# ScalarE's counters opened first, and the C factors of all blocks formed at once, in the front of a two-block sequence kernel

## The chip, the cores and the metric

One core of a Trainium2 chip (trn2) runs the whole kernel. The time is the device time of one execution in microseconds; the number compared is the median over runs. The engines are named PE (TensorE), DVE (VectorE), ACT (ScalarE), POOL (GpSimd) and SP (SyncE, which only issues DMAs here); "PEld" is PE's loading of weights.

## What is computed

A sequence of 512 tokens of width 1024 passes through two stacks of two layers. The change touches the start of the first layer, a state-space mixer, whose core is

```python
hn = rmsnorm(h, norm_mix[0])
dt = exp(log_dt)[:, None]; mag = exp(lam_re * dt)
a_r = mag * cos(lam_im * dt); a_i = mag * sin(lam_im * dt)
coef = ((a_r - 1) + 1j * a_i) / (lam_re + 1j * lam_im)   # coef_r, coef_i
bb = coef * (b_re + 1j * b_im)                            # 64 groups x 64 states x 16
# per group: s[t] = a * s[t-1] + bb @ hn[t];  y[t] = Re(c @ s[t])
y = gelu(y + d * hn); a, b = split(y @ w_glu); mix = a * sigmoid(b)
```

What follows (the gated feed-forward layers, windowed attention, a second stack with a second state-space layer and differential attention) isn't touched; it is 289 weight units of 128 x 1024 that stream from HBM while PE multiplies.

## The kernel before

Everything is written in one program, with one instruction stream for each engine and semaphores between them. There is no planner: each engine executes its list in the order of the code, and a wait stops all that stands behind it on that engine. `Steps` is a counter: a semaphore with a list of names, each of which is one increment a turn. So that the waits for a turn before the first are met, every counter has to be opened: `open(e)` adds 4 turns in advance. The engine that makes a counter's steps opens it.

The front works on 64 groups in 8 blocks (NBLK) of 8 groups (GB). The recurrence over 512 tokens is cut into 64 pieces (NSTEP) of 8 steps (STEP): tables with the powers 0 to 8 of each group's factor carry eight steps at once, and a scan over the 64 pieces does the rest.

- **Powers.** `s5_vector` (DVE) forms dt, the turns, and PB, the powers 0 to 8 of all groups (L578 to L604); ACT does the exponentials and sines in between (`s5_scalar`, L482 to L488). psi (L604) releases `psi_ready`, for which POOL waits.
- **B side.** DVE multiplies the first block's B by the norm's gain (L651); POOL does so for the other seven blocks, 896 elements twice (L453). `tables(q)` in `s5_vector` forms TB of block q (L614, L622, L623, L622, L623), and waits for `s5_k` "K2" of block q-1: TB is a single buffer, and PE's `direct(q-1)` reads it.
- **C side.** `c_powers(lo, hi)` (L635 to L647) forms TA, the factors of C, for a range of groups, in six instructions: L641, L642 and L644 and L645 read two operands in SBUF; L643 and L646 have one in PSUM. Before the change it is called for the first block (72 elements an instruction) and, behind U, for the other seven (504 elements). Each call ends with an increment of `tables_ready`. POOL's `tables(q)` (L427, L428, L429; 1152 elements each) forms TC of block q; the first waits for `tables_ready` 1, all others for 2.
- **The picked norm.** ACT squares h (L493), PE sums over the partitions (L739), ACT takes the root sd (L244). DVE picks from sd what each of the eight steps needs (L671, L673, L674) as ru, and U = Ur * ru of block 0 (L678). For blocks 1 to 7 POOL forms U (`inputs`, L434), and SP reloads Ur (L409) once U of the block before is done.
- **Angles.** POOL's `angles(q)` (L438) forms psi x piece number; DVE takes the fraction (`fractions`, L632, L633), ACT the sines and cosines (L500 to L504). `angles(0)` waits for psi, for the constants, and for the counter `s5_angles`, which ACT opens.
- **Blocks.** On DVE a block is L700, L702, L703, the scan L707, L709, `direct` (L689), L714, L716, then `tables` and `fractions` of the next one. On PE: `transposed` (L749), `step_sums` (L768: U through the turned tables), `rotated` (L774, needs ACT's copy L521 of the sums), `direct` (L759, needs TC), then outputs (L812, L813) and the turn of the scan's result (L795).

POOL's list at the start is: wait for psi; `angles(0)`; gain B; wait for C; `tables(0)`; then for T from 0: `tables(T + 1)`, `inputs`, `angles(T + 1)`.

Of the kernel before, what the change touches and what calls it, by code (L numbers as in the profile page):

```python
# [14 lines left out]
SG, SH, SN = 64, 16, 64  # L15
STEP = 8
NSTEP = TOK // STEP
GB = LANES // SH
# [74 lines left out]
def program(nc, a):  # L93
    ctx = ExitStack()
    with ctx:
# [10 lines left out]
        def sem(name):  # L106
            return ctx.enter_context(nc.semaphore(name))
# [30 lines left out]
        def V(name, lo=0, hi=None, rows=LANES):  # L138
            a0, a1 = PC[name]
            return par[0:rows, a0 + lo:(a1 if hi is None else a0 + hi)]  # L140
# [48 lines left out]
        def act_split(e, v0, n4):  # L189

            if isinstance(n4, int) and v0 + 4 * n4 >= UNITS:
                return
            z = v0 % RING
            e.wait_ge(raw_loaded[z], n4 * 16 + (v0 // RING + 1) * 16)
            e.activation(w_hi[:, z], raw[:, z], ACT.Copy).then_inc(hi_split, 1)  # L195
# [44 lines left out]
        def act_norm(e, n, eps):  # L240
            e.wait_ge(norm_mm, n + 1)
            if n:
                e.wait_ge(r_ready, n)
            e.activation(sd[:, :], bk[4], ACT.Sqrt, bias=eps[:, :], scale=1.0 / DM).then_inc(sd_ready, 1)  # L244
# [101 lines left out]
        s5_kept = Steps(sem("s5_kept"), "Sx", ahead=4)  # L346
        s5_st_kept = Steps(sem("s5_turned_kept"), "ST1 ST2", ahead=4)
        s5_k_kept = Steps(sem("s5_direct_kept"), "K1 K2", ahead=4)
        s5_angles = Steps(sem("s5_angles"), "absf sin cos", ahead=4)
        s5_y_kept = Steps(sem("s5_y_kept"), "Y1 Y2", ahead=4)  # L350
        s5_gelu = Steps(sem("s5_gelu"), "hi g", ahead=4)
# [10 lines left out]
        def link(e, ins):  # L362

            chain[0] += 1
            ins.then_inc(vec_chain, 1)
            e.wait_ge(vec_chain, chain[0])
# [16 lines left out]
        def cut(t, q, width=GB):  # L383

            return t[:, q * width:(q + 1) * width]
# [91 lines left out]

        def s5_scalar(e):
            s = small
            flat = lambda t: t[:, :, :].rearrange("p g s -> p (g s)")  # L480
            e.wait_ge(par_loaded, 16)
            e.activation(s["dt"][:, :], V("log_dt"), ACT.Exp).then_inc(dt_ready, 1)  # L482
            e.wait_ge(magnitudes, 1)
            e.activation(flat(power["mag"]), flat(power["mag"]), ACT.Exp).then_inc(magnitudes, 1)
            e.wait_ge(power_steps, 1)
            e.activation(flat(power["sin"]), flat(power["turns"]), ACT.Sin, scale=SIN_SCALE).then_inc(trig_ready, 1)
            e.wait_ge(power_steps, 2)
            e.activation(flat(power["cos"]), flat(power["whole"]), ACT.Sin, bias=half_pi[:, :], scale=-SIN_SCALE).then_inc(trig_ready, 1)  # L488
            e.wait_ge(h_loaded, 16)
            for m in range(KT):  # L490
                if m >= 4:
                    e.wait_ge(acc_ready, m - 3)
                e.activation(squares[m % 4], h[:, m], ACT.Square).then_inc(squared, 1)  # L493
            act_norm(e, 0, eps6)

            def turned(t):
                z = t % 2
                e.wait_ge(s5_phases.sem, s5_phases.at("f", t))
                e.wait_ge(s5_angles.sem, s5_angles.at("cos", t - 1))
                s5_angles.took("absf", e.activation(absf, ff, ACT.Abs))  # L500
                e.wait_ge(s5_states.sem, s5_states.at("po2", t - 2))
                s5_angles.took("sin", e.activation(sinb[:, z], ff, ACT.Sin, scale=SIN_SCALE))
                e.wait_ge(s5_angles.sem, s5_angles.at("absf", t))
                s5_angles.took("cos", e.activation(cosb[:, z], absf, ACT.Sin, bias=half_pi[:, :], scale=-SIN_SCALE))  # L504

            def st_kept(t):
                e.wait_ge(s5_sums.sem, s5_sums.at("S", t - 1))
                for k in (1, 2):
                    e.wait_ge(s5_tt.sem, s5_tt.at(f"ST{k}", t))
                    s5_st_kept.took(f"ST{k}", e.activation(ST[:, 4 * k - 4:4 * k, :], bk[k - 1].rearrange("p (g n) -> p g n", g=4), ACT.Copy))  # L510

            def k_kept(t):
                e.wait_ge(t_loaded[t % 2], 16 * STEP * (t // 2 + 1))
                for k in (1, 2):
                    e.wait_ge(s5_k.sem, s5_k.at(f"K{k}", t))
                    s5_k_kept.took(f"K{k}", e.activation(Ksb[:, t % 2, 4 * k - 4:4 * k, 1:, :], kbank(k)[:, :, 1:, :], ACT.Copy))

            def s_kept(t):
                e.wait_ge(s5_sums.sem, s5_sums.at("S", t))
                e.wait_ge(s5_js.sem, s5_js.at("JS", t - 2))  # L520
                s5_kept.took("Sx", e.activation(Sx[:, t % 2], grid(bank[2]), ACT.Copy))  # L521

            def step(T):
                if 0 <= T < NBLK:
                    st_kept(T)
                    if T == 0:
                        turned(T)
                        s_kept(T)
                    k_kept(T)
                q = T - 2  # L530
                if 0 <= q < NBLK:
                    e.wait_ge(s5_turned.sem, s5_turned.at("YT", q))
                    tok = bk[7].rearrange("p (s c) -> p s c", s=STEP)
                    s5_gelu.took("hi", e.activation(cut(x1h, q, 1).rearrange("p o (c s) -> p (o s) c", s=STEP), tok, ACT.Gelu_apprx_tanh))
                    e.wait_ge(s5_low.sem, s5_low.at("lo", q - 1))
                    s5_gelu.took("g", e.activation(a32[:, :], bk[7], ACT.Gelu_apprx_tanh))
                if 0 < T < NBLK:
                    s_kept(T)
                    turned(T)
                q = T - 1  # L540
                if 0 <= q < NBLK:
                    e.wait_ge(s5_turned.sem, s5_turned.at("YT", q - 1))
                    for k in (1, 2):
                        e.wait_ge(s5_out.sem, s5_out.at(f"Y{k}", q))
                        s5_y_kept.took(f"Y{k}", e.activation(Ysb[:, :, 4 * k - 4:4 * k, :].rearrange("p s g h -> p g s h"), ybank(k).rearrange("p (g s h) -> p g s h", g=4, s=STEP), ACT.Copy))
                if 3 <= T < 6:
                    act_split(e, T - 3, 0)
            for counters in (s5_kept, s5_st_kept, s5_k_kept, s5_angles, s5_y_kept, s5_gelu):
                counters.open(e)
            for T in range(NBLK + 2):  # L550
                step(T)
            e.wait_ge(par_rest, 16)
            e.wait_ge(const_rest, 16)
            e.sem_inc(x_hi, 8)

        def kbank(k):
            return bank[5][64 * (k - 1):64 * (k - 1) + SH, :].rearrange("p (g s h) -> p g s h", g=4, s=STEP)

        def ybank(k):
            return bank[4][64 * (k - 1):64 * k, :]  # L560

        def s5_vector(e):
# [72 lines left out]
            def c_powers(lo, hi):  # L635

                p0, p1 = PB[:, 0, lo:hi], PB[:, 1, lo:hi]
                wr, ci = over(v("w")[:, lo:hi]), over(v("ci")[:, lo:hi])
                m0, m1 = (b[:, 0:(hi - lo) * (STEP + 1)].rearrange("p (g s) -> p g s", s=STEP + 1) for b in (bank[6], bank[7]))
                t0, t1 = TA[:, 0, lo:hi], TA[:, 1, lo:hi]  # L640
                link(e, tt(m0, p0, wr, ALU.mult))  # L641
                link(e, tt(t0, p1, ci, ALU.mult))  # L642
                link(e, tt(t0, m0, t0, ALU.add))  # L643
                link(e, tt(m1, p0, ci, ALU.mult))  # L644
                link(e, tt(t1, p1, wr, ALU.mult))  # L645
                link(e, tt(t1, t1, m1, ALU.subtract))  # L646
                e.sem_inc(tables_ready, 1)  # L647
# [14 lines left out]
            link(e, tt(v("c2"), v("nr"), v("g2"), ALU.mult))  # L662
            link(e, tt(v("ci"), v("c3"), v("c2"), ALU.subtract))
            c_powers(0, GB)
            link(e, ts(mag8[:, :], mag[:, :, STEP], 1.0, None, ALU.mult))
            e.wait_ge(const_loaded, 16)
            fractions(0)
# [8 lines left out]
            e.sem_inc(ru_ready, 1)  # L676
            e.wait_ge(u_loaded, 16)
            s5_inputs.took("U", tt(Ub[:, 0], Ur[:, :, :], ru[:, :].unsqueeze(1).to_broadcast(full), ALU.mult))  # L678
            c_powers(GB, SG)
            dg = bank[7][0:SH, 0:SG]  # L680
            link(e, tt(dg, V("d_h", rows=SH), V("gain_u", rows=SH), ALU.mult))
            dfull = [SH, SG, SH]
# [1907 lines left out]
```

## Time and profile before

| | |
|---|---|
| Median of 3 runs | 2085.6 us (2083.46 to 2087.68) |
| Profiled execution | 2085.45 us, span 2083.7 us |
| PE busy | 1944.7 us (93%) |
| DVE busy | 1279.2 us (61%) |
| ACT busy | 898.9 us (43%) |
| POOL busy | 433.5 us (21%) |
| Mean granted clock of PE | 0.973 |
| PE busy in each of the first four slices of 52 us, in tenths | 3, 8, 7, 9 |
| PE's granted clock in these slices, in tenths | 7, 8, 9, 9 |

The profile is of one execution. A row of the time order gives the start, the length, engine and line, what is written and read with shapes, and in brackets how long the engine had been idle before it and what released it. A length includes time in which the instruction had begun and was held up. Where a row says "x8", it is eight instructions in a row. PE is busy nearly everywhere but in the first 160 us, the front, where the work is handed from engine to engine.

### The profile page before, as it was taken

To read this page: it belongs to the slowest core of one execution; us is meant where nothing else is said; L and a number is where in the kernel's file an instruction comes from. 1 tells how busy PE (TensorE), PEld (TensorE's weight loads), DVE (VectorE), ACT (ScalarE), POOL (GpSimd) and SP (SyncE) were. 2 spreads that over 40 slices of the span, in tenths; PEclk is the share of its full clock that TensorE was granted. 3 is DMA by queue.
4 is the path that set the end of the run, shared out by engine and by line. 5 is a ranking of instruction groups with operands and counts; after the bars stand their busy time and mean duration, and the time that the engine had idled before them with its cause. 6 is when DMAs were issued, how large, how long until landed. Compare 5 with 4: busy or idle time off the path is not lost.

```text
span 2083.7 us, 27291 instructions
## 1 busy us (share of the span) xinstructions
PE 1944.7 (93%) x9494; PEld 1564.5 (75%) x9494; DVE 1279.2 (61%) x1783; ACT 898.9 (43%) x1503; POOL 433.5 (21%) x295
## 2 busy tenths in 40 slices
PE   3879999999999967999999999999999998999996
PEld 2668788888887745788888887878878886777774
DVE  7984443433469587543343468987667765777764
ACT  3674432332335255432232333445445552466661
POOL 4772200000044010300000044352212224100003
PEclk7899999999999979999999999999999999999998
DMA  4213333333332200332333332222222222222221
GB/s 178 45 33 108 94 91 101 93 98 99 93 99 84 84 6 11 91 100 91 101 93 99 96 96 81 81 61 63 70 79 64 71 71 62 91 62 62 70 71 61
DMA packets 54522, 166.98 MB, mean 80 GB/s; under 512 B 13216, under 2 KB 13344, under 8 KB 53920
## 3 DMA queue, kind: packets, MB, share of 16 engines
q1 hardware_dynamic: 54432, 165.78, 26.6%
q8 instruction: 56, 0.92, 0.2%
q14 instruction: 34, 0.28, 0.0%
HBM read 161.30 MB, written 2.10 MB: 78 GB/s over the span
## 4 chain that ended last, share of the span: by engine, by line
PE 74%; DVE 12%; ACT 5%; POOL 3%; issue 3%; DMA 2%; DVEq 0%; POOLq 0%; SPq 0%; PEldq 0%
PE bank L183 15%; PE bank L184 15%; PE bank L185 15%; PE bank L1478 3%; PE bank L1479 3%; PE bank L1480 3%; DMA raw<-in_w_dram 2%; PE bank L2084 2%; PE bank L2086 2%; PE bank L2085 2%; PE bank L1493 1%; POOL acc L234 1%; PE bank L1494 1%; PE bank L1495 1%; ACT w_hi L195 1%
## 5 line engine op out<-in xcount | busy, mean ns | idle before, releaser
L203 DVE TENSOR_TENSOR w_lo<-raw,w_hi 128x1024 fp32r<-128x1024 f32 x286 | 367.2, 1284 | 460.8 <-ACT w_hi L195 459.4
L195 ACT ACTIVATE w_hi<-raw 128x1024 fp32r<-128x1024 f32 x289 | 305.8, 1058 | 627.2 <-DMA raw<-in_w_dram 627.2
L183 PE MATMUL bank<-x1h,w_hi 128*128 128x512 f32 x744 | 291.6, 392 | 6.6 <-DVE x1l L218 6.6
L185 PE MATMUL bank<-x1h,w_lo 128*128 128x512 f32 x744 | 289.7, 389 | 0.0
L184 PE MATMUL bank<-x1l,w_hi 128*128 128x512 f32 x744 | 289.7, 389 | 0.0
L183 PE MATMUL bank<-x0h,w_hi 128*128 128x512 f32 x704 | 277.9, 395 | 0.0
L185 PE MATMUL bank<-x0h,w_lo 128*128 128x512 f32 x704 | 274.1, 389 | 0.0
L184 PE MATMUL bank<-x0l,w_hi 128*128 128x512 f32 x704 | 274.0, 389 | 0.0
L232 POOL TENSOR_TENSOR sq<-h 128x512 f32 (+1 forms) x64 | 79.0, 1234 | 784.0 <-DVEq L917 660.4
L183 PEld LDWEIGHTS bank<-x1h,w_hi 128*128 128x128 f32 x744 | 139.7, 188 | 38.1 <-DVE x1l L218 7.9
L184 PEld LDWEIGHTS bank<-x1l,w_hi 128*128 128x128 f32 x744 | 139.8, 188 | 29.3 <-issue 0.7
L185 PEld LDWEIGHTS bank<-x1h,w_lo 128*128 128x128 f32 x744 | 139.8, 188 | 29.1
L1478 PE MATMUL bank<-x1h,w_hi 128*128 128x512 f32 x384 | 155.9, 406 | 0.0
L183 PEld LDWEIGHTS bank<-x0h,w_hi 128*128 128x128 f32 x704 | 132.2, 188 | 29.8 <-issue 2.5
L184 PEld LDWEIGHTS bank<-x0l,w_hi 128*128 128x128 f32 x704 | 132.2, 188 | 29.3 <-issue 2.3
L185 PEld LDWEIGHTS bank<-x0h,w_lo 128*128 128x128 f32 x704 | 132.1, 188 | 27.5
L1479 PE MATMUL bank<-x1l,w_hi 128*128 128x512 f32 x384 | 151.1, 393 | 0.0
L1480 PE MATMUL bank<-x1h,w_lo 128*128 128x512 f32 x384 | 150.9, 393 | 0.0
L234 POOL TENSOR_TENSOR acc<-acc,sq 128x512 f32<-128x512 f32 x64 | 102.5, 1602 | 5.0
L896 DVE TENSOR_TENSOR x1l<-a,x1h 128x512 f32 x64 | 44.3, 693 | 92.7 <-ACT a L886 92.7
L884 ACT ACTIVATE x1h<-t 128x512 f32 x64 | 40.5, 632 | 130.7 <-DVE t L894 130.7
L1478 PEld LDWEIGHTS bank<-x1h,w_hi 128*128 128x128 f32 x384 | 73.1, 190 | 18.1 <-issue 1.9
(379 smaller groups left out, 3464.7 us busy)
## 6 DMA issues: line engine op xcount, KB each, us to landing
raw<-in_w_dram SPq DMA_DIRECT2D x289, 512.0 KB, 3.5
h<-in_xT_dram SPq DMA_DIRECT2D x1, 2048.0 KB, 12.6
Ur<-in_xu_dram SPq DMA_DIRECT2D x8, 256.0 KB, 2.7
out_dram<-h SPq DMA_DIRECT2D x8, 256.0 KB, 2.2
const<-in_const_dram SPq DMA_DIRECT2D x1, 1028.0 KB, 14.6
B_st<-in_B_dram SPq DMA_DIRECT2D x1, 1024.0 KB, 6.8
C_st<-in_C_dram SPq DMA_DIRECT2D x1, 1024.0 KB, 14.6
p_in<-in_pT_dram SPq DMA_DIRECT2D x1, 1024.0 KB, 5.1
```

The lines of the kernel that those rows point to most:

```text
L183: e.matmul(b, w_hi[:, w, k], xh[:, k], start=(k == 0), stop=False)
L184: e.matmul(b, w_hi[:, w, k], xl[:, k], start=False, stop=False)
L185: last = e.matmul(b, w_lo[:, w, k], xh[:, k], start=False, stop=(k == KT - 1))
L195: e.activation(w_hi[:, z], raw[:, z], ACT.Copy).then_inc(hi_split, 1)
L203: e.tensor_tensor(w_lo[:, z], raw[:, z], w_hi[:, z].bitcast(F32), ALU.subtract).then_inc(w_split, 1)
L232: e.tensor_tensor(one(sq[:, :]), tile(h, m), tile(h, m), ALU.mult).then_inc(squared, 1)
L234: e.tensor_tensor(acc[:, :], acc[:, :], sq[:, :], ALU.add).then_inc(acc_ready, 1)
L896: e.tensor_tensor(tile(x1l, m), one(a32[:, :]), tile(x1h, m).bitcast(F32), ALU.subtract).then_inc(a_ready, 1)
L1478: e.matmul(b, w_hi[:, w, k], x1h[:, k], start=(k == 0), stop=False)
L1479: e.matmul(b, w_hi[:, w, k], x1l[:, k], start=False, stop=False)
L1480: last = e.matmul(b, w_lo[:, w, k], x1h[:, k], start=False, stop=(k == KT - 1))
L2084: e.matmul(b, w_hi[:, w, k], xh[:, k], start=(k == 0), stop=False)
```

## The change

ScalarE opens its six counters as the first thing it does, instead of after the norm's root. And DVE forms the C factors of blocks 1 to 7 (`c_powers(GB, SG)`) right after those of block 0, instead of behind U of block 0: ahead of the copy mag8 (L665), the fractions of block 0 and the picked norm.

```diff
@@ s5_scalar(e):
             s = small
+            for counters in (s5_kept, s5_st_kept, s5_k_kept, s5_angles, s5_y_kept, s5_gelu):
+                counters.open(e)
             flat = lambda t: t[:, :, :].rearrange("p g s -> p (g s)")
             e.wait_ge(par_loaded, 16)
...
                 if 3 <= T < 6:
                     act_split(e, T - 3, 0)
-            for counters in (s5_kept, s5_st_kept, s5_k_kept, s5_angles, s5_y_kept, s5_gelu):
-                counters.open(e)
             for T in range(NBLK + 2):
                 step(T)
@@ s5_vector(e):
             c_powers(0, GB)
+            c_powers(GB, SG)
             link(e, ts(mag8[:, :], mag[:, :, STEP], 1.0, None, ALU.mult))
             e.wait_ge(const_loaded, 16)
             fractions(0)
...
             s5_inputs.took("U", tt(Ub[:, 0], Ur[:, :, :], ru[:, :].unsqueeze(1).to_broadcast(full), ALU.mult))
-            c_powers(GB, SG)
             dg = bank[7][0:SH, 0:SG]
```

No instruction is added or removed.

## Rows read from the trace of the kernel before

**Rows 1.** The page: the span of the profiled execution.

```profile
span 2083.7 us, 27291 instructions
```

**Rows 2.** The chain of work that ended last: start us, length us, engine, output, line.

```profile
30.97 0.89 DVE Ub L678
...
56.06 1.54 DVE Zb L707 x8
```

**Rows 3.** POOL in order of time, 0 to 75 us: start, length, instruction, idle before.

```profile
25.75 1.04 POOL L438 TENSOR_TENSOR R<-psi,const 128x512 f32<-128x512 f32 x1 [23.20 <-ACTq L64]
26.75 4.56 POOL L453 TENSOR_TENSOR B_st<-B_st,gain_row 128x896 f32<-128x896 f32 x2
31.27 2.59 POOL L427 TENSOR_TENSOR TC<-C_st,TA 128x1152 f32<-128x1152 f32 x1
...
36.47 2.94 POOL L429 TENSOR_TENSOR TC<-TC,TCt 128x1152 f32<-128x1152 f32 x1
41.53 2.14 POOL L427 TENSOR_TENSOR TC<-C_st,TA 128x1152 f32<-128x1152 f32 x1 [2.12 <-DVEq L647]
```

**Rows 4.** DVE in order of time, 0 to 75 us.

```profile
12.75 0.43 DVE L651 TENSOR_TENSOR B_st<-B_st,gain_row 128x256 f32<-128x256 f32 x1 [0.23 <-DVE psi L604]
13.21 1.23 DVE L614 TENSOR_TENSOR TB<-B_st,PB 128x1024 f32<-128x1024 f32 x1
14.35 0.69 DVE L622 TENSOR_TENSOR bank<-B_st,PB 128x512 f32<-128x512 f32 x1
...
21.18 0.22 DVE L665 TENSOR_SCALAR mag<-s_mag 128x64 f32<-128x64 f32 x1 [0.16 <-DVE TA L646]
...
28.26 1.13 DVE L671 TENSOR_TENSOR bank<-sd,const 128x512 f32<-128x512 f32 x1
...
30.27 0.55 DVE L674 RECIPROCAL ru<-ru 128x64 f32<-128x64 f32 x1
...
31.78 2.62 DVE L641 TENSOR_TENSOR bank<-PB,s_w 128x504 f32<-128x504 f32 x1
...
40.71 0.68 DVE L646 TENSOR_TENSOR TA<-TA,bank 128x504 f32<-128x504 f32 x1
41.55 2.21 DVE L681 TENSOR_TENSOR bank<-par 16x64 f32<-16x64 f32 x1 [0.15 <-DVE TA L646]
...
45.03 1.94 DVE L614 TENSOR_TENSOR TB<-B_st,PB 128x1024 f32<-128x1024 f32 x1
46.89 3.10 DVE L622 TENSOR_TENSOR bank<-B_st,PB 128x512 f32<-128x512 f32 x1
...
69.80 0.70 DVE L702 TENSOR_TENSOR bank<-bank,sinb 128x512 f32<-128x512 f32 x1 [1.38 <-PE bank L774]
```

**Rows 5.** ACT in order of time, 25 to 26.5 us.

```profile
25.33 0.69 ACT L244 ACTIVATE sd<-bank,eps 128x512 f32<-128x512 f32 x1 [1.59 <-PEq L741]
```

**Rows 6.** DMA: C on the page, then Ur's tile, 0 to 60 us.

```profile
C_st<-in_C_dram SPq DMA_DIRECT2D x1, 1024.0 KB, 14.6
...
DMA to landing us min/median/max: 2.6/3.5/13.0
```

**Rows 7.** DVE in order of time: two one-source instructions, early and late.

```profile
4.92 0.20 DVE L583 TENSOR_SCALAR s_k<-s_k 128x64 f32<-128x64 f32 x1
...
1854.83 1.07 DVE L2237 TENSOR_SCALAR s2t_nm<-s2t_mx 128x2 f32<-128x2 f32 x1
```

**Rows 8.** POOL in order of time, 1805 to 2012 us.

```profile
1854.57 1.31 POOL L2332 TENSOR_TENSOR ol<-OT,oh 128x512 fp32r<-128x512 f32 x1 [77.65 <-ACT oh L2284]
```

**Rows 9.** PE in order of time, 0 to 75 us.

```profile
31.91 3.67 PE L768 MATMUL bank<-Ub,ST 128*128 128x64 f32 x16 [5.28 <-DVE Ub L678]
36.28 2.07 PE L774 MATMUL bank<-Sx,const 128*128 128x512 f32 x2 [0.69 <-ACT Sx L521]
39.46 2.72 PE L759 MATMUL bank<-TC,TB 128*16 128x128 f32 x16 [1.11 <-POOL TC L429]
```

**Rows 10.** PE in stretches of 0.2 us: us, busy (x), clock, DMA share, GB/s.

```profile
67.80:68.00 0.20, 0.20 (x3) 0.51 0.00 0
```

## The prediction

> **What bounds the kernel now.** The program spans 2083.7 us [rows 1]; all that the change touches happens in its first 60. I read the chain of work first: it says which part of the front can give or cost time. From 30.97 us, where VectorE scales the first block's input (U, L678), to the scan of block 0 that ends at 57.60 us, nearly every piece is VectorE's [rows 2]; the scan L707 is in the chain again in each later block. So a delay of the scan of block 0 is a delay of the end: weight loads, splits and the PE-bound remainder all follow in relative order.
>
> Second, POOL's row of time. It sat idle 23.20 us until ScalarE's queue (L64, the counters' increment) let it start L438 at 25.75, then gained B for 4.56 us, then formed the first block's C tables (L427 to L429) from 31.27 and the second's from 41.53 [rows 3]. The reader is to see that all this work is dammed up behind one increment.
>
> Third, VectorE's row beside it [rows 4]. L641 takes 2.62 us, L622 3.10 us, and L681, of 16x64 elements, 2.21 us; L622 alone at 14.35 took 0.69. The long ones read both sources from SBUF while POOL is at work, and end just after POOL's instruction ends: L427 ends at 31.27 + 2.59 = 33.86, L641 at 34.40; L453 ends at 31.31, U at 31.86 [rows 2 to 4]. So one of the two engines waits out the other's whole instruction, and VectorE then needs another 0.54 us for 512 elements (0.08 for the 64 of L681, some 1.08 for the 1024 of L614: 1.23 - 0.69 + 0.54). It is mutual: the second L453 ends 31.31 - 29.39 = 1.92 us after L671 let it go, and L427 33.86 - 31.86 = 2.00 us after U; free, it takes 2.14 [rows 3, 4]. For L429, 2.94 less some 0.45 of waiting is 2.5. The two alternate. L646, with a source in PSUM, takes 0.68 beside POOL [rows 4].
>
> The Trainium skill (SBUF — State Buffer, section "Who interferes with whom") says the same: a VectorE instruction with two SBUF inputs and a GpSimd instruction that reads SBUF block each other wholly, in order of issue. It speaks against this change, which starts POOL sooner.
>
> **The counters opened first.** The six increments move ahead of ScalarE's wait for the parameters and cost nothing on the path. The transposes no longer wait for them behind sd (25.33 + 0.69 = 26.02 [rows 5]), worth nothing, as U comes later. POOL is now released when psi is ready, at 12.75 - 0.23 = 12.52 us [rows 4]: it starts L438 at 12.67 (it woke 0.14 us after L646's end at 41.39 [rows 3, 4]), ending 13.71, against VectorE's gain L651, ready at 12.75. L651 ends 13.98; POOL's first L453 15.90; L614 16.98; the second L453 18.90; the first L622 19.44, where it ended at 15.04 before. From there POOL waits for the C powers and VectorE runs free. Cost: **+4.4 us** up to this point. Before, it was hidden: VectorE idled for the angles until 26.9 anyhow. C lands 14.6 us after its issue [rows 6], which is among the first on SP's queue: in time.
>
> **The C powers ahead.** The small powers ended at 21.18 - 0.16 = 21.02, now 25.42. This starts POOL's tables(0) at 25.56 (5.7 us earlier), and the large powers at 25.58. They took 31.78 to 41.39 = 9.6 us, six instructions worth some 4.3 free, the rest waiting for exactly these POOL instructions [rows 3, 4]. The same company is there now: L427 25.56 to 27.70, L641 to 28.24; from L641's end to L646's took 41.39 - 34.40 = 6.99, so L646 ends at 35.23. Moving them removes no contention.
>
> **What now stands before U.** The increment after L646 wakes POOL for tables(1) at 35.37; the copy L665 (mag8) starts at 35.38. L665 reads one source, SBUF to SBUF. No such copy stands beside POOL in the front, so I bound it: 0 more if it does not wait (the reciprocal L674, also of one source, ran its 0.55 us within L453 [rows 3, 4]), 2.1 if it waits out L427. The nearest row is of its own operation: L2237, of 2 elements, began at 1854.83 within POOL's L2332 (from 1854.57, 1.31 long) and took 1.07, ending 0.02 after it [rows 7, 8]. I take the wait. What speaks against it is that L665's source is strided: its 0.22 us [rows 4] is more than L583's 0.20 for as many contiguous elements [rows 7], so it could run in another form.
>
> The Trainium skill (VectorE: DVE Perf Modes, section "Mode 2×_2P — use both read ports for one tensor") wants for the two-port mode only SBUF on both sides and an even outermost dimension, 64 here, and no unit stride. By that L665 waits: 2092.3 below; by a strided form that does not wait, 2089.6.
>
> L665 ends at 37.6; the two fractions instructions (1.4) at 39.0; L671 waits for L428 (37.6 + 2.14 = 39.73) and ends at 40.3; from L671's end to U's start took 30.97 - 29.39 = 1.58 [rows 2, 4], so U stands ready at 41.87, waits for L429 (40.3 + 2.5) and ends at **43.3**, against 31.86: **+11.4**. ScalarE's angles of block 0, behind the fractions, are done by then and have room.
>
> **From U to tables(1).** TB is a single buffer: tables(1) on VectorE waits until PE's direct(0) has read TB. PE's chain from U: 31.91 step sums, 36.28 turn (after ScalarE's copy), 39.46 direct(0), done at 42.18, of which 1.1 was a wait for POOL's TC [rows 9], gone now. So 31.86 to 42.18 less 1.15 is 9.2: direct(0) is done at 43.3 + 9.2 = **52.5**. Before, L614 started at 45.03, led by VectorE itself with 2.9 us to spare; now PE leads it. This is the wait that takes the place of the powers: VectorE has nothing left but L681 and L683 (to 44.7) and then idles.
>
> POOL: tables(1) ends at 42.8; inputs(1) needs the reload of Ur, which SP issues behind U (landing 2.6 at the least [rows 6]): 46.0 to 47.3 (L438, of equal size, takes 1.04 free; the L434 in this place 1.3); angles(1) to 48.35; then tables(2), three instructions from 48.35: L427 to 50.5, L428 to 52.7. L614 arrives at 52.5 and ends 52.7 + 1.08 = 53.8; L429 takes it to 56.3; the first L622 ends at **56.8**. Before it ended at 46.89 + 3.10 = 49.99 [rows 4]: tables(1) met POOL both times. Difference **+6.8 us**. The rest up to the scan of block 0 had no waits for POOL before and has none after. POOL has done tables(2) earlier, so that L709 is shorter by up to 1.8, but PE, from this scan on, sets the next step: L702 waited 1.38 us for PE's turn [rows 4], and does so again.
>
> **The sum.** The profiled execution took 2085.45 us (span 2083.7 and 1.75 around it); the median of the three runs is 2085.6. 2085.45 + 6.8 = **2092.2**, 0.32% over the median.
>
> **The rivals.** (1) *The wait of L665 does not happen.* U ends at 40.6, direct(0) at 49.8, tables(2) on POOL starts at 45.6, and the first L622 ends at 54.05: +4.1, 2089.6. For it: the strided source. Chance 0.12, half of it above 0.2%.
>
> (2) *PE's clock.* The granted clock is at its lower level, 0.5 (1.2 GHz), in the whole stretch from 31 to some 68 us [rows 10], and L768's 16 matmuls take 3.67 us [rows 9]. After the change PE's first burst is without the 1.1 us hole. Should it rise in it and stay, PE's step after the scan shortens and VectorE can gain the 1.38 and the shorter L709: some 2.8, so +4.0, 2089.5. It speaks against it that VectorE's idle time leaves PE idle for some 5 us after direct(0). Chance 0.13, half below 0.2%.
>
> (3) *The change does what it seems to be after:* VectorE and POOL overlap freely where they were not seen together, in the gaining of B and the early tables(0). The powers take 4.3 us from 21.2 and end near 25.5, before sd (26.02 [rows 5]); fractions, L671 to L674 and U end near 30.3; direct(0) is done at 39.5; tables(1) takes 3.5 us free and ends at 43.1, where it ended near 52.4: -9.3, 2076. It decides if L614 at 14.0 does not wait for L453. Everything in [rows 3, 4] speaks against. With partial forms of it (-4 and more) chance 0.12.
>
> (4) *Partly absorbed*, 0 to +4: POOL in another rhythm, for instance free when L622 comes (it then ends at 54.4 or sooner). Chance 0.10.
>
> (5) *More than forecast:* Ur lands 3.5 us after its issue [rows 6], POOL's L428 ends at 53.5, and the first L622 at 57.6: +7.6, and with one POOL instruction more in VectorE's way up to +9.5, 2095. Chance of over +8: 0.08.
>
> **How the numbers follow.** Forecast (+6.3 to +8) 0.45, rivals 0.12, 0.13, 0.12, 0.10, 0.08. The range 2086.8 to 2095.0 holds the forecast, rivals 1 and 2, half of 4 and most of 5: about 0.8. About 0.2% is what a measurement of this kernel can tell from no change, here 4.2 us. Slower: 0.45 + 0.06 + 0.06 + 0.08 = 0.65; faster 0.12; within 0.2%: 0.23.
>
> **What the profile after would show.** POOL's L438 at 12.7 instead of 25.75; L614 of 3.0 and L622 of 2.4 us near 14 to 19.5; POOL's first L427 near 25.6; L665 of 2.2 us; U near 43; L614 of tables(1) near 52.5 with an idle time ended by PE's L759; the first block's scan near 64. L665 of 0.2 us would be rival 1; L614 of 1.2 us at 14 rival 3; a granted clock of 1.0 before 60 us rival 2. The prediction is wrong if tables(1) starts before 45 us, or if the shift at the first scan isn't found at the end.

## The result, and the profile after

The changed kernel took 2093.66 us, median of 7 runs (2089.85 to 2095.42), against 2086.56 for the kernel before (7 runs): a ratio of 1.0028, 95% interval 1.0015 to 1.0041. It is slower, as forecast, and inside the range; the forecast was 2092.2. The profiled execution spans 2091.9 us, 8.2 more than [rows 1].

The page of the changed kernel, its first lines:

```profile
span 2091.9 us, 27291 instructions
...
PE 1948.7 (93%) x9494; PEld 1570.5 (75%) x9494; DVE 1284.5 (61%) x1783; ACT 898.9 (43%) x1503; POOL 434.5 (21%) x295
```

Some lines of code have moved by one or two: L665 is now L666, L671 is L672, L678 is L679, L504 is L506. POOL in order of time, the counterpart of [rows 3] (start, length, instruction, idle before and its releaser):

```profile
12.64 1.04 POOL L438 TENSOR_TENSOR R<-psi,const 128x512 f32<-128x512 f32 x1 [10.09 <-DVEq L605]
13.64 5.27 POOL L453 TENSOR_TENSOR B_st<-B_st,gain_row 128x896 f32<-128x896 f32 x2
25.63 2.65 POOL L427 TENSOR_TENSOR TC<-C_st,TA 128x1152 f32<-128x1152 f32 x1 [6.72 <-issue]
...
35.22 2.14 POOL L427 TENSOR_TENSOR TC<-C_st,TA 128x1152 f32<-128x1152 f32 x1 [1.39 <-DVEq L647]
```

POOL starts 13.1 us sooner. DVE in order of time, the counterpart of [rows 4]:

```profile
12.72 1.23 DVE L651 TENSOR_TENSOR B_st<-B_st,gain_row 128x256 f32<-128x256 f32 x1 [0.23 <-DVE psi L604]
13.99 2.98 DVE L614 TENSOR_TENSOR TB<-B_st,PB 128x1024 f32<-128x1024 f32 x1
16.89 2.58 DVE L622 TENSOR_TENSOR bank<-B_st,PB 128x512 f32<-128x512 f32 x1
...
25.59 0.69 DVE L641 TENSOR_TENSOR bank<-PB,s_w 128x504 f32<-128x504 f32 x1 [0.16 <-DVE TA L646]
26.32 2.50 DVE L642 TENSOR_TENSOR TA<-PB,s_ci 128x504 f32<-128x504 f32 x1
...
35.24 2.19 DVE L666 TENSOR_SCALAR mag<-s_mag 128x64 f32<-128x64 f32 x1 [0.16 <-DVE TA L646]
...
41.72 1.43 DVE L679 TENSOR_TENSOR Ub<-Ur,ru 128x512 f32<-128x512 f32 x1 [0.15 <-DVEq L677]
...
52.44 1.23 DVE L614 TENSOR_TENSOR TB<-B_st,PB 128x1024 f32<-128x1024 f32 x1 [7.91 <-PE bank L759]
53.58 3.11 DVE L622 TENSOR_TENSOR bank<-B_st,PB 128x512 f32<-128x512 f32 x1
...
62.53 1.53 DVE L707 TENSOR_TENSOR_SCAN Zb<-mag,bank 128x64 f32<-128x64 f32 x8
...
74.56 0.70 DVE L702 TENSOR_TENSOR bank<-bank,sinb 128x512 f32<-128x512 f32 x1 [1.39 <-PE bank L774]
```

The reader is to see three things. POOL's L438 (12.64 to 13.68 us) stretches L651 by 0.80 us, and its two instructions that gain B stretch L614 and L622 by 1.75 and 1.89, 4.4 together. The copy mag8 takes 2.19 us where it took 0.22. And DVE idles for 7.91 us before tables(1), released by PE's L759: the wait that took the place of the powers. The scan of block 0 starts at 62.53, 6.5 us later than in [rows 2].

The chain of work that ended last (start, length, what) shows the same hand-over to PE between U and tables(1):

```profile
41.72 1.44 DVE Ub L679
...
43.20 3.69 PE bank L768 x16
...
46.92 0.60 ACT Sx L523
...
47.57 2.07 PE bank L774 x2
49.64 2.60 PE bank L759 x15
```

**Where the 8.2 us of the profile are.** I followed three marks through both traces: the start of the scan of block 0, the start of block 1's scan, and POOL's memset L226 that starts the norm in the GLU. They stand at 56.06, 71.26 and 163.01 us before and at 62.53, 76.03 and 172.80 after: later by 6.5, 4.8 and 9.8 us. At the last norm the shift is 8.2. So the front up to the scan explains 6.5; PE's step behind it gave back 1.7; the stretch from block 1's scan to the GLU took 5.0 more; and some 1.6 came back after it. The stretch from 60 to 170 us, PE alone, of before and then of after (us, busy (x), granted clock, DMA share, GB/s):

```profile
60.00:170.00 110.00, 91.57 (x670) 0.96 0.17 38
```

```profile
60.00:170.00 110.00, 96.05 (x647) 0.85 0.17 37
```

The mean granted clock there is 0.85 instead of 0.96; it drops to 0.5 (1.2 GHz) for part of several blocks. From scan to scan the kernel before has a clock of 1.00 everywhere behind its second scan. The changed kernel has 0.76 from the third scan to the fourth (14.2 us instead of 13.4), 0.75 from the fifth to the sixth (13.7 instead of 13.5) and 0.60 from the seventh to the eighth (12.2 instead of 10.4). The two stretches that follow the last two of these are at 1.00 and 0.99 and still take 0.6 and 1.7 us more, so over 2 of the 5.0 us fall behind a low stretch and not in it. At the last block, where DVE waits for PE's sums and ACT's angles, the row of L700 shows it: it had waited 4.15 us before and 5.73 after, and PE's step sums had taken 3.52 us at the lower level where they take 1.9 at the upper.

```profile
155.32 0.69 DVE L700 TENSOR_TENSOR tA<-bank,cosb 128x512 f32<-128x512 f32 x1 [5.73 <-ACT cosb L506]
```

### The profile page after: what moved, and what is told of

Same layout as the page of the kernel before. It is cut to its first block, busy times and chain, and to the rows that moved or that the text cites. A ratio compares the mean times of both kernels' runs of the same rounds, so it can differ in the third digit from the quotient of the medians.

```text
span 2091.9 us, 27291 instructions
## 1 busy us (share of the span) xinstructions
PE 1948.7 (93%) x9494; PEld 1570.5 (75%) x9494; DVE 1284.5 (61%) x1783; ACT 898.9 (43%) x1503; POOL 434.5 (21%) x295
## 4 chain that ended last, share of the span: by engine, by line
PE 74%; DVE 11%; ACT 5%; issue 3%; POOL 3%; DMA 2%; DVEq 0%; POOLq 0%; SPq 0%; PEldq 0%
PE bank L183 15%; PE bank L185 15%; PE bank L184 15%; PE bank L1478 3%; PE bank L1480 3%; PE bank L1479 3%; DMA raw<-in_w_dram 2%; PE bank L2084 2%; PE bank L2086 2%; PE bank L2085 2%; POOL acc L234 1%; PE bank L1493 1%; PE bank L1494 1%; PE bank L1495 1%; ACT w_hi L195 1%
## 6 DMA issues: line engine op xcount, KB each, us to landing
const<-in_const_dram SPq DMA_DIRECT2D x1, 1028.0 KB, 14.2
```

## The experiments

All columns but the last are read from one profile of each kernel; "scan" is the start of block 0's scan, "GLU mark" the start of L226. The last column compares the medians with the kernel before on the same chip, over 7 to 12 runs of the kernel and 7 to 31 of the kernel before.

| Kernel | U ends | Scan of block 0 | GLU mark | Scan to mark | Clock, 60 to 170 us | Ratio to before (95%) |
|---|---|---|---|---|---|---|
| before | 31.86 | 56.06 | 163.01 | 106.95 | 0.96 | 1 |
| changed | 43.15 | 62.53 | 172.80 | 110.27 | 0.85 | 1.0028 (1.0015 to 1.0041) |
| changed, again | 43.17 | 62.56 | 170.44 | 107.88 | 0.88 | 1.0031 (1.0016 to 1.0046) |
| counters only | 30.89 | 52.18 | 159.14 | 106.96 | 0.98 | 0.9978 (0.9962 to 0.9994) |
| powers only | 31.48 | 52.89 | 165.33 | 112.44 | 0.89 | 0.9990 (0.9974 to 1.0007) |
| copy mag8 ahead | 40.78 | 60.23 | 165.51 | 105.28 | 0.97 | 1.0009 (0.9989 to 1.0029) |
| release after both | 35.27 | 53.35 | 159.48 | 106.13 | 0.95 | 0.9971 (0.9954 to 0.9989) |
| B gained later | 37.85 | 58.10 | 168.15 | 110.05 | 0.88 | 1.0002 (0.9987 to 1.0016) |
| all three | 31.86 | 52.90 | 165.30 | 112.40 | 0.87 | 0.9969 (0.9952 to 0.9986) |
| split gain | 32.07 | 50.16 | 158.18 | 108.02 | 0.94 | 0.9985 (0.9969 to 1.0002) |
| before, delayed | 32.32 | 64.41 | 176.14 | 111.73 | 0.82 | 1.0050 (1.0032 to 1.0067) |
| changed, filler | 43.17 | 62.62 | 166.86 | 104.24 | 0.96 | 1.0017 (1.0000 to 1.0035) |
| before, filler | 31.66 | 55.86 | 162.93 | 107.07 | 1.00 | 0.9991 (0.9972 to 1.0010) |

### Each part alone

Counters only (the second part undone):

```diff
             s = small
+            for counters in (s5_kept, s5_st_kept, s5_k_kept, s5_angles, s5_y_kept, s5_gelu):
+                counters.open(e)
```

> The kernel before with only the counters opened first; the large C powers stay behind U. Theory (VectorE and POOL wait out each other's whole instructions): the gaining of B still meets tables(0) and costs 4.4 us, but then U of block 0 ends near 33.4 us (31.9 before, 43.2 in the changed kernel), the powers behind it run free in 4.3 us instead of 9.6, and the scan of block 0 ends near 55 us, some 2.4 earlier than before (57.6; changed kernel 64.1). Rival (early POOL work is what costs, whatever the place of the powers): the scan ends 4 to 6 us later than before, at 62 or later. Whole time by the theory -2 us against before, give or take what PE's granted clock does later; by the rival +4 or more.

Measured: the scan starts at 52.18, 3.9 us earlier than before, and the whole is faster by 0.22% (2083.46 against 2087.85 us). The rival falls: early POOL work alone does not cost. DVE in order of time:

```profile
16.85 2.58 DVE L622 TENSOR_TENSOR bank<-B_st,PB 128x512 f32<-128x512 f32 x1
...
25.56 0.22 DVE L665 TENSOR_SCALAR mag<-s_mag 128x64 f32<-128x64 f32 x1 [0.16 <-DVE TA L646]
...
29.94 0.95 DVE L678 TENSOR_TENSOR Ub<-Ur,ru 128x512 f32<-128x512 f32 x1 [0.15 <-DVEq L676]
30.81 3.11 DVE L641 TENSOR_TENSOR bank<-PB,s_w 128x504 f32<-128x504 f32 x1
33.95 0.68 DVE L642 TENSOR_TENSOR TA<-PB,s_ci 128x504 f32<-128x504 f32 x1
```

The 4.4 us at B are paid here too, but in time that was idle. I had U end at 33.4 and it ended at 30.9: the copy mag8 began at 25.56, 0.03 before POOL's L427 (25.59), and so escaped. Behind U the powers ran nearly free: one wait of 2.4 us instead of 5.3 in all.

Powers only (the first part undone):

```diff
             c_powers(0, GB)
+            c_powers(GB, SG)
...
-            c_powers(GB, SG)
             dg = bank[7][0:SH, 0:SG]
```

> The kernel before with only the large C powers moved ahead; the counters are opened late, so that POOL stands still until 25.75 us. Theory: tables(0) on VectorE ends at 17.2 as before, the powers run free from 21.2 to 25.5 us (no instruction over 0.8 us), fractions and U stay where they were (U ends near 31.9), direct(0) is done near 41.1, and the scan of block 0 ends near 55 us, 2.5 earlier than before. Rival (the powers ahead of the norm delay U and with it everything): U ends near 36 and the scan near 62. Whole time by the theory -2.5 us against before, by the rival +4.

Measured: the powers ran free from 21.19 to 25.48, U ended at 31.48, and the scan started at 52.89, 3.2 us earlier than before. The copy mag8 was caught by L438, which ran from 25.38 to 26.42:

```profile
25.63 0.87 DVE L666 TENSOR_SCALAR mag<-s_mag 128x64 f32<-128x64 f32 x1 [0.16 <-DVE TA L646]
```

The whole is not to be told from before (0.9990): in its profile the stretch from scan to GLU took 112.4 us at a clock of 0.89, which ate the 3.2. That is one execution, 2.1 us above the median of its ten.

So each part alone brings the scan 3 to 4 us forward, and both together put it 6.5 us back. Together they start POOL's tables(0) at the very moment of the large powers, with U behind them. And both spend the same idle time of DVE, which before stood ahead of the fractions of block 0:

```profile
26.92 0.69 DVE L632 TENSOR_SCALAR bank<-R 128x512 f32<-128x512 f32 x1 [5.52 <-POOL R L438]
```

The 4.4 us at B fit into these 5.5 alone, and so do 4.3 us of powers without waits; together they don't.

### Which meeting costs what

The copy ahead of the powers, in the changed kernel:

```diff
+            link(e, ts(mag8[:, :], mag[:, :, STEP], 1.0, None, ALU.mult))
             c_powers(0, GB)
             c_powers(GB, SG)
-            link(e, ts(mag8[:, :], mag[:, :, STEP], 1.0, None, ALU.mult))
```

> The changed kernel with the copy mag8 moved ahead of both calls of the C powers, so that it no longer stands beside POOL's tables(1). Theory (the strided one-source copy waits out L427, 2.19 us in the changed kernel's profile, and U behind it then misses one more POOL instruction): U ends near 40.7 instead of 43.2, the scan of block 0 starts near 59.9 instead of 62.5. Rival (the 2.2 us would have been waited anyway at the next two-source instruction): the scan starts at 62 to 62.5.

Measured: U at 40.78 and the scan at 60.23, 2.3 us earlier than in the changed kernel (2.6 expected). A copy of 64 elements costs 2.3 us of the front by its place; the rival falls.

POOL released after both calls:

```diff
                 link(e, tt(t1, t1, m1, ALU.subtract))
-                e.sem_inc(tables_ready, 1)
...
             c_powers(GB, SG)
+            e.sem_inc(tables_ready, 2)
```

> The changed kernel with POOL's tables(0) released only after both calls of the C powers. Theory: the large powers run free (4.3 us instead of 9.6, from 25.6 to 29.9), POOL's tables(0) starts near 30 instead of 25.6, U ends near 37.9, and the scan of block 0 starts near 58.1 (62.5 in the changed kernel). Rival (the later tables(0) on POOL holds back PE's direct(0) by as much as the powers gain): the scan starts at 62 or later.

Measured: the powers ran free from 25.51 to 29.79, and the scan started at 53.35, 9.2 us earlier than in the changed kernel (4.4 expected). The mechanism held, its size was twice mine: the copy mag8 began at 29.95, 0.03 before POOL's L427 (29.98), and escaped as well, so that U ended 7.9 us earlier (5.3 expected), and DVE's tables(1) met POOL in a better rhythm (L622 1.75 us instead of 3.11). The whole is 0.29% faster than before, though the 4.4 us at B are still in it.

B gained on POOL after its tables(0):

```diff
             angles(0)
-            e.wait_ge(g_loaded, 16)
...
             tables(0)
+            e.wait_ge(g_loaded, 16)
+            e.wait_ge(b_loaded, 16)
+            for part in range(2):
+                tt(B_st[:, part, GB:], B_st[:, part, GB:], gain_row[:, GB:], ALU.mult).then_inc(b_gained, 1)
```

> The changed kernel with POOL's gaining of B for blocks 1 to 7 moved behind its tables(0). Theory: VectorE's tables(0) meets only L438 and ends near 18.1 instead of 21.65, but L453 then stands beside the end of the large powers and the copy mag8; U ends near 38, the scan of block 0 starts near 59.1, 3.4 earlier than in the changed kernel. Rival (the waiting only moves to where L453 went): the scan starts at 62 or later.

Measured: L614 took 1.22 us at 14.04 again, U ended at 37.85 and the scan started at 58.10, 4.4 us earlier (3.4 expected). U gained 5.3 us: 3.6 at L614 and L622, 1.0 at the copy mag8, which now stood beside L453 and took 1.14 instead of 2.19, and the rest at L672 and U itself. POOL's gaining of B, now from 30.20 to 34.75 us, makes DVE wait some 0.9 us at the copy and 0.5 at L672.

All three together, the three diffs above in one kernel:

> The changed kernel with all three: the copy mag8 ahead, POOL's tables(0) released after both calls, B gained on POOL after tables(0). Theory: the large powers run free and end near 26.5, U ends near 32, the scan of block 0 starts near 53.4, 9 us before the changed kernel and 2.6 before the kernel before; the whole time lies some 3 us under the kernel before, give or take PE's granted clock. Rival (the early release of POOL isn't worth anything once it has been spread out; counters alone are as good): the scan starts no earlier than in the kernel with the counters alone, 52.2. Both can hold; a scan later than 56 would speak against the theory of the waits.

Measured: U at 31.86, the scan at 52.90 (53.4 expected), 9.6 us before the changed kernel, the whole 0.31% faster than before (2083.36 against 2090.07 us). It isn't earlier at the scan than the counters alone (52.18), so this part of the rival holds too: once U stands at 31 to 32, the next thing late is tables(1) against POOL's tables(1), where L614 took 2.58 and L622 3.10 us.

This kernel and the late release split the 11.3 us by which U is late in the changed kernel. The late release takes away 7.9, most of what the meetings with tables(0) and tables(1) cost. The other 3.4 go when the waits at B go as well: 4.4 at B and 4.3 of powers are 3.2 more than the idle 5.5 us.

### The carry to the end

The kernel before with a pure delay:

```diff
+            for again in range(6):
-            link(e, tt(DI[:, :, :], ...
+                link(e, tt(DI[:, :, :], ...
```

> The kernel before with VectorE's product DI (L683) written six times instead of once, with the same values, just ahead of tables(1): a pure delay of some 6.2 us on VectorE in the place where the changed kernel is late, with POOL and the C powers as they were. Theory (a shift of the scan of block 0 is carried to the end): the scan starts near 62.5 us as in the changed kernel, and the median lies 5 to 7 us over the kernel before, like that of the changed kernel. Rival (the changed kernel's excess comes from something else of it, and the front has slack of its own): the scan is late but the median lies within 2 us of the kernel before.

Measured: the scan at 64.41, 8.4 us late where some 6.4 were expected (the six writes took 7.44, and tables(1) then met POOL three times), and the median 9.2 us over the kernel before (2097.18 against 2088.03), a ratio of 1.0050. A delay of the first scan without any of the change is carried to the end. The rival falls.

The changed kernel, unaltered:

> The changed kernel, unaltered, beside the others on one chip. Theory: the first scan starts at 62.5 us again, since nothing up to there depends on chance; from the scan to the GLU it takes between 104 and 112 us, the more the longer the granted clock is low in between, so that the median comes out 4 to 8 us over the kernel before. Rival (the low stretches of its first profile belong to the change): from scan to GLU it takes 110 us again.

Measured: U at 43.17 and the scan at 62.56, within 0.03 us of the first profile; the GLU mark at 170.44, 2.4 us earlier than there; the median 5.4 us over before. Up to the scan the two profiles agree. From scan to mark it took 107.9 us this time and 110.3 the first, so at least this difference isn't the change's own.

That a shift is carried to the end doesn't say that all of it arrives. With the copy ahead the scan is 4.2 us late and the median 0.45 under the kernel before, at a ratio of 1.0009 with an interval from 0.9989 to 1.0029; with all three the scan is 3.2 early and the median 6.7 under.

### The clock

The filler, one product that nothing reads, in the changed kernel and in the kernel before:

```diff
                 if 0 <= q < NBLK:
+                    e.matmul(bank[5][32:48, :], C("ident", hi=16), h[:, 0], start=True, stop=True)
                     e.wait_ge(s5_states.sem, s5_states.at("Z", q))
```

> The changed kernel with one more 128x16 by 512 product on PE in each block of the front, into a part of a PSUM bank that nothing reads, just before PE's wait for the scan (an idle stretch). Theory of the clock (of the 8.2 us between the two profiles only 4.8 stand at the second block, the rest comes from stretches at the lower granted clock in blocks 3 to 8): with the filler the granted clock stays at 1.0 from the third block to the GLU, and the GLU's start (POOL's memset L226) is near 168 us instead of 172.8 (163.0 before). Rival (the later 5 us have another cause, a queue or a weight load): the clock may rise, the GLU still starts near 172 or later.

> The kernel before with the same filler. It was at clock 1.0 from 68 us on in its profile, so by the theory of the clock its front changes by under 1 us there, GLU's start near 163, and its runs spread less; if the filler itself is in the way it starts 0.5 us later for each of the blocks, near 167.

Measured: in the changed kernel the scan stood where it was (62.62), and the GLU mark came at 166.86 (168 expected), 5.9 us earlier than in the first profile and 3.6 earlier than in the second; the mean granted clock from 60 to 170 us was 0.96, not 1.0 throughout: two of the stretches from scan to scan had 0.87 and 0.88. In the kernel before, where the clock was up anyhow, the mark stayed (162.93). That speaks for the clock as what the blocks lose. The other profiles agree: the stretch from the last scan to the mark took 13.7 us in the seven where the one ahead of it had a clock of 1.00, and 14.1 to 15.7 in the six where that had 0.60 to 0.71. But no median gained by it: 1.0017 for the one, inside the interval of the changed kernel, and 0.9991 for the other, whose ten runs also spread no less than those of the kernel before (standard deviation 3.9 us against 3.5). In both profiles the attention stage behind, between the third L226 (611.57 us in the kernel before) and the fourth (829.80), took longer: 220.7 and 222.7 us, where the kernels without the filler took 217.1 to 220.1. The code there is the same, and the mean granted clock of that stage was 0.92 in both, as in the kernel before, which took 218.2. So what the filler gave in the front was lost elsewhere or wasn't there in the other runs, and the cause stays open.

Over the runs, too, time and clock go together. In 24 runs of the kernel before on the chip of the repeated run, the correlation of time with the mean granted clock is -0.79, and each 0.001 of clock goes with some 1.5 us; in the changed kernel's 12 runs there -0.78 and 1.4. At one clock, 0.972, the fitted lines give 2088.2 and 2092.3 us. By this estimate 4 us are what the change costs apart from the clock, and 1 to 3 us of the measured difference go with a slightly lower clock (0.9704 against 0.9721 in the mean); whether that is a consequence of the change or chance stays open. The line is a correlation and no price: with the filler the kernel before had a mean clock of 0.9752 instead of 0.9716 in the runs beside it, by the slope there (1.2 us) some 4 us, and its median was 0.6 us lower.

### A version that beats both

The gaining of B split: DVE does blocks 0 and 1 in one instruction, POOL the other six after its angles(1), on top of all three changes of order:

```diff
-            link(e, tt(B_st[:, :, 0:GB] ... gain_row[:, 0:GB] ...
+            link(e, tt(B_st[:, :, 0:2 * GB] ... gain_row[:, 0:2 * GB] ...
...
                 if 0 <= T + 1 < NBLK:
                     angles(T + 1)
+                if T == 0:
+                    for part in range(2):
+                        tt(B_st[:, part, 2 * GB:], ... gain_row[:, 2 * GB:], ALU.mult).then_inc(b_gained, 1)
```

> Built on the kernel with all three changes of order: VectorE gains B for blocks 0 and 1 itself, in one instruction of 512 elements, and POOL gains the other six blocks only after its angles(1), so that its tables(1) follows tables(0) at once and is over when VectorE's tables(1) begins. Theory of the waits: U ends near 32 us, POOL's tables(1) near 41.3, VectorE's tables(1) starts near 41.3 and meets only L434 and L438; the scan of block 0 starts near 50.5 us, 12 earlier than in the changed kernel, 5.5 than before, and the median lies 4 to 6 us under the kernel before. Rival (PE's clock and its own step set the end, the scan of block 0 no longer does): the scan is earlier but the median stays where that of the kernel with all three was, some 3 us under the kernel before or less.

Measured: the scan at 50.16 (50.5 expected), the earliest of all, but the median only 3.5 us under before (2084.53 against 2088.03), 0.9985 with an interval that reaches 1.0002. The first two scans were 5.9 and 6.4 us earlier than before, the GLU mark 4.8. The 12.4 us to the changed kernel at the first scan are 8.9 in the medians. The rival fits better here: the last gain at the scan isn't to be seen in the median, though the kernel with all three ran on another chip, beside other runs of the kernel before. The kernels with the counters alone, with the late release and with all three are shown faster than the kernel before; between them the runs don't decide.

## Why the prediction was right

**What bounds.** Right: the front's chain over DVE carried the delay, as the delayed kernel shows.

**The counters first.** Right to the tenth: L438 at 12.64 (12.67), L651, L614 and L622 ending at 13.95, 16.97 and 19.47 (13.98, 16.98 and 19.44), +4.4 us.

**The powers ahead.** Right in the sum, wrong in the detail. I had POOL begin first at 25.56; DVE began at 25.59 and POOL at 25.63, so L641 went free with 0.69 and L645 (2.97) paid later. L646 ended at 35.08 against 35.23. Who is first by 0.03 us changed which instruction waits, not how much all of them wait.

**The copy mag8.** Taken as waiting, by the row of L2237; it took 2.19 us. Moved away it gave 2.3 us. The Trainium skill's rule (VectorE: DVE Perf Modes, section "Mode 2×_2P — use both read ports for one tensor"), by which the strided source is no hindrance, holds in this case: 2.19 us beside L427 and 0.87 beside L438. Rival 1 did not come. What I didn't see is how thin the choice is: in two other kernels the same copy began 0.03 us before POOL and took 0.22.

**U and tables(1).** U at 43.15 (43.3), direct(0) done near 52.3 (52.5), first L622 ended at 56.69 (56.8), scan +6.5 (+6.8). I had misread one thing: behind the first L622 I saw no more waits for POOL before the change, but the second L622 took 0.92 us at 50.75 before and 0.70 now, which is 0.2 of the 0.3 that were missing at the scan.

**The carry.** This is the step that was only half right. I let PE's step behind the scan be as before. It was shorter, because the granted clock was up for part of it: L795 took 1.13 us instead of 2.07, L768 2.96 instead of 3.51, and block 1's scan was only 4.8 late. That is half of rival 2. The clock did rise at the end of PE's first burst (1.00 from 52.2 us), but it fell again at 55.4 with PE idle, as its objection had it, and rose once more from 62.3 to 65.6. In the repetition it stayed up from there, and block 1's scan was only 3.2 late. Windows of the changed kernel, PE alone (us, busy (x), clock, DMA share, GB/s):

```profile
53.00:56.00 3.00, 0.00 (x0) 0.91 0.00 0
...
61.00:64.00 3.00, 1.55 (x13) 0.79 0.34 66
64.00:67.00 3.00, 2.88 (x15) 0.78 0.41 109
67.00:70.00 3.00, 3.00 (x15) 0.50 0.39 77
```

Then it was down for parts of later blocks, which no term of the sum held, and these came out 5.0 longer. In the profile the two, with the 1.6 that came back behind the GLU, made 8.2 out of 6.5; over the runs the change cost 7.1 by the medians and 5.4 in the repetition. The forecast of +6.8 lies between them, in part by luck: the front's term was sound, and one for the later blocks and the clock, of either sign and up to 5 us in the profile, was missing. It belonged in the range, and the range held it only because it was made wide for other reasons.

**Rival 3**, free overlap, fell with every row; rivals 4 and 5 did not come.

## What to carry to other kernels

A wait that keeps an engine idle may also keep it out of another engine's way: before removing it, list the two-source SBUF instructions that the woken engine will now run beside, and count up to one whole instruction of waiting for each. Two changes of order that each bring the critical step forward can put it back together, because they meet or because they spend the same idle time, so try each alone. Release a neighbour just after the stretch in which the two would wait for each other, and keep even the smallest copy out of the place where the neighbour has just been woken.

## What the runs showed that I had not expected

- The order between two engines that become ready within 0.03 us decides 2 us: the copy mag8 took 0.22 us when it began at 25.56 and 29.95 against POOL's 25.59 and 29.98, and 2.19 us when it began at 35.24 against 35.22.
- The clock's level can differ between two executions of one program whose first scans start within 0.03 us of each other: near 66 us it fell to the lower level in the first profile of the changed kernel and stayed at the upper in the second. From the first scan to the GLU mark it took 104.2 to 108.0 us in the seven profiles whose mean clock from 60 to 170 us was 0.94 or more, and 107.9 to 112.4 in the six at 0.82 to 0.89.
- Over whole executions, 0.001 of mean granted clock goes with 0.8 to 1.7 us of this kernel's time in the sets of runs, so two kernels that differ by 4 us can be told apart in ten runs only just.
